# Strassen-form MLP kernel on one core: the last group's last two products made block by block, and three halves of the last norm finished on ScalarE and GpSimd

## The chip, the cores and the metric

The kernel runs on one core of one Trainium2 chip. The metric is the device time of one execution, in microseconds (us). Engines are named as the profile names them: PE is the matrix engine (TensorE) and PEld its weight loads, DVE is VectorE, ACT is ScalarE, POOL is GpSimd, and SP issues the DMA transfers. All times inside an execution are counted from the first instruction of the profiled one.

## What is computed

One layer of a decoder trunk on 512 positions of width 1024, all in float32: three mixers, their gated merge and projection, a first layer norm, then the part that matters here, an MLP with squared ReLU and a second layer norm.

```python
x = _layer_norm(ALPHA * x + mixed, ln1_g, ln1_b)
h = jnp.square(jax.nn.relu(jnp.einsum('bsd,df->bsf', x, w_up)))
x = _layer_norm(ALPHA * x + jnp.einsum('bsf,fd->bsd', h, w_down), ln2_g, ln2_b)

def _layer_norm(x, g, b):
    mu = jnp.mean(x, axis=-1, keepdims=True)
    var = jnp.mean(jnp.square(x - mu), axis=-1, keepdims=True)
    return (x - mu) * lax.rsqrt(var + LN_EPS) * g + b
```

## The kernel before

**Numbers in two parts.** A float32 matmul is made as three matmuls of values split into a high and a low part (`three`, L1246 to L1250). ACT writes the high part of a weight slab, DVE subtracts to get the low part, and PE waits for the low part (`slab`).

**The down product.** The 512 positions are four blocks of 128 (b = 0 to 3), and the 1024 output columns are two halves of 512 (e = 0, 1). Residual and output live in `resid[:, b, half]`. The hidden width of 4096 is worked through in four groups (g = 0 to 3). In each group the down product is a Strassen form with seven products in the order `PRODUCTS`, that is m1, m5, m6, m3, m2, m7, m4. Each product has two row blocks (r = 0, 1), and each row block is one call of `down_part`: four pairs times three matmuls, 12 matmuls of 512 columns. It is written here as "m7,0" for product m7, row block 0.

**Sums in PSUM.** A product that is not in `DOWN_OPENS` goes on adding to the bank that the product before it left: m1, m6, m7 and m4 share bank 4 + r. After each part DVE adds the bank, or subtracts it, into a half of the residual (`down_add`, L1148). So m4,r may not start before DVE has read what m7,r left (`LAST_READ`, `down_ready`: `pe.wait_ge(down_read, made(g, LAST_READ[name], r))`). `made` numbers the parts in the order in which PE makes them, and DVE reads them in that same order. By `down_add`, m3 goes into half 1 of blocks 2 and 3 and m2 into their half 0; m7 goes into half 1 of blocks 0 and 1 and m4 into their half 0.

**The last norm.** In the last group `half_stats` takes the statistics of a half as soon as it is final (L1154). `norm_two(n, b)` then finishes a block: aggregate the statistics (L1157), subtract the mean and multiply with the gain for each half (L1160), take the reciprocal of the standard deviation, of which ACT made the root (L633), then multiply with it and add the bias for each half (L1165). The blocks are finished in the order 2, 3, 0, 1, all on DVE. SP stores each half, 256 KB, in that order (L394).

**Order.** Each engine runs its own instructions strictly in the order in which they are written; there are no priorities. Counting semaphores order the engines among each other.

Of the kernel before, what the change touches and what calls it, by code (L numbers as in the profile page):

```python
# [20 lines left out]
ALU = mybir.AluOpType  # L21
# [8 lines left out]
WID = 512  # L30
# [49 lines left out]

def made(g, name, r):

    return 2 * len(PRODUCTS) * g + 2 * PRODUCTS.index(name) + r + 1


def down_slab(g, name):
# [36 lines left out]
def build(nc, x, mem, lower_bounds, w_in, conv_w, hg_norm_w, w_mem_k, w_mem_v, w_branch, b_gate, w_o,  # L123
          ln1_g, ln1_b, w_up, w_down, ln2_g, ln2_b, out):
    ds = bass.ds
    with ExitStack() as ctx:
# [3 lines left out]
        def sem(name):  # L130
            return ctx.enter_context(nc.semaphore(name))
# [119 lines left out]
        h_squared, form_step, forms_made = sem("h_squared"), sem("form_step"), sem("forms_made")  # L251
        forms_hi, forms_ready = sem("forms_hi"), sem("forms_ready")
        kept_hi, kept_ready = sem("kept_hi"), sem("kept_ready")
        down_done, down_read = sem("down_done"), sem("down_read")

        OPERANDS = 10


        def proj_round(half):
# [53 lines left out]
        def _(sp):  # L313
# [57 lines left out]
            for g in range(G_MLP):  # L371
# [15 lines left out]
                up_load(g, 2)  # L387
                up_load(g, 3)
                direct(g, 4, down_block(g, 2, 1), PAIRS)
            for n, b in enumerate((2, 3, 0, 1)):  # L390
                for e in range(2):
                    part = slice(e * WID, (e + 1) * WID)
                    sp.wait_ge(y_ready, 2 * n + (e + 1))
                    sp.dma_start(out_t[b][:, part], resid[:, b, part]).then_inc(stored, 16)  # L394
            sp.wait_ge(stored, 16 * 2 * TB)


        @block.gpsimd
        def _(pool):
            chain = [0]  # L400

            def after(ins):

                ins.then_inc(pool_chain, 1)
                chain[0] += 1
                pool.wait_ge(pool_chain, chain[0])

            after(pool.memset(ident[:], 0.0))
            pool.affine_select(out=ident[:], in_=ident[:], compare_op=ALU.not_equal, fill=1.0, base=0,
                               pattern=[[-1, P]], channel_multiplier=1).then_inc(ident_ready, 1)  # L410
            after(pool.memset(ones_f, 1.0))
            pool.tensor_copy(ones[:], ones_f)
            pool.memset(scan_keep[:], 1)
            pool.memset(eps[:, 0:1], LN_EPS)
            pool.memset(eps[:, 1:2], RMS_EPS)
            pool.memset(sc_causal, 0.0)
            pool.memset(decays[:, :, 0:1], 1.0)
            after(pool.memset(causal_f, 0.0))

            pool.memset(scan_keep[:].rearrange("p (n c) -> p n c", c=C)[:, :, 0:1], 0)  # L420

            after(pool.affine_select(out=causal_f, in_=causal_f, compare_op=ALU.is_gt, fill=1.0, base=0,
                                     pattern=[[-1, P]], channel_multiplier=1))
            pool.tensor_copy(causal[:], causal_f).then_inc(consts_ready, 1)

            for half in range(2):
                def parts(src, high, low, n, ready):
                    pool.tensor_copy(high, src).then_inc(half_hi, 1)
                    pool.wait_ge(half_hi, n)
                    pool.tensor_tensor(low, src, high.bitcast(F32), ALU.subtract).then_inc(ready, 1)  # L430

                if half == 0:
                    for t in range(4):
                        main_copied(pool, 0, t)
                else:
                    pool.wait_ge(aux_done, HALF.done("as3", half - 1))
                parts(mem_k[:, 2 * half:2 * half + 2, :], mk_hi, mk_lo, 2 * half + 1, khalf_ready)
                if half == 0:  # L440
                    for t in range(4, 8):
                        main_copied(pool, 0, t)
                else:
                    pool.wait_ge(aux_done, HALF.done("pv1", half - 1))
                parts(mem_v[:, :, half * 256:(half + 1) * 256], mv_hi, mv_lo, 2 * half + 2, vhalf_ready)

            pool.wait_ge(branch_split, 8)
            pool.memset(merged, 0.0).then_inc(merge_done, 1)

            for b in range(TB):  # L450
                pool.wait_ge(aux_done, LNT.done("x%d1" % b))
                pool.tensor_scalar(resid[:, b, :], resid[:, b, :], ALPHA, 1.0, ALU.mult, ALU.mult)\
                    .then_inc(resid_ready, 1)


        @block.scalar
        def _(act):
# [249 lines left out]
            def mlp(g):  # L707
                if g == 0:
                    up_hi(0, 2)
                up_hi(g, 3)  # L710
                for j in range(PAIRS):
                    even_tile(g, j)
                    odd_tile(g, j)
                    if j < 3:
                        down_hi(g, PRODUCTS[j])
                    forms_to_hi(g, j)
                down_hi(g, "m3")
                down_hi(g, "m2")
                act.activation(form_hi[:, FORM_OF["m4"], :], h_kept.rearrange("p j t -> p (j t)"), ACT.Copy)\
                    .then_inc(kept_hi, 1)  # L720
                down_hi(g, "m7")
                down_hi(g, "m4")
                if g < G_MLP - 1:
                    for j in range(3):
                        up_hi(g + 1, j)
                else:
                    for n in range(TB):
                        norm(TB + n)

            for g in range(G_MLP):  # L730
                mlp(g)
# [3 lines left out]
        def _(dve):  # L735
# [286 lines left out]
            def half_of(b, e):  # L1022
                return resid[:, b, e * WID:(e + 1) * WID]
# [129 lines left out]
                dve.wait_ge(down_read, made(g, name, r))  # L1153
                ln_link(dve.bn_stats(half_two(b, e), half_of(b, e)))  # L1154

            def norm_two(n, b):
                dve.bn_aggr(mv[:], both_two(b)).then_inc(var_ready, 1)  # L1157
                dve.wait_ge(var_ready, TB + n + 1)
                for e in range(2):
                    dve.scalar_tensor_tensor(half_of(b, e), half_of(b, e), mv[:, 0:1],  # L1160
                                             ln_par[:, 2, e * WID:(e + 1) * WID], ALU.subtract, ALU.mult)
                dve.wait_ge(std_ready, TB + n + 1)
                ln_link(dve.reciprocal(lnw[:, 1:2], lnw[:, 0:1]))
                for e in range(2):
                    dve.scalar_tensor_tensor(half_of(b, e), half_of(b, e), lnw[:, 1:2],  # L1165
                                             ln_par[:, 3, e * WID:(e + 1) * WID], ALU.mult, ALU.add)\
                        .then_inc(y_ready, 1)

            def mlp(g, last):
                if g == 0:  # L1170
# [19 lines left out]
                down_lo(g, "m7")  # L1190
                down_add(g, "m6", 1)
                down_add(g, "m3", 0)
                if last:
                    half_stats(g, "m3", 0)
                down_lo(g, "m4")
                down_add(g, "m3", 1)
                if last:
                    half_stats(g, "m3", 1)
                else:
                    up_lo(g + 1, 0)  # L1200
                down_add(g, "m2", 0)
                if last:
                    half_stats(g, "m2", 0)
                    norm_two(0, 2)
                down_add(g, "m2", 1)
                if last:
                    half_stats(g, "m2", 1)
                else:
                    up_lo(g + 1, 1)
                for r in range(2):  # L1210
                    down_add(g, "m7", r)
                if last:
                    norm_two(1, 3)
                    half_stats(g, "m7", 0)
                    half_stats(g, "m7", 1)
                else:
                    up_lo(g + 1, 2)
                for r in range(2):
                    down_add(g, "m4", r)
                    if last:  # L1220
                        half_stats(g, "m4", r)
                        norm_two(2 + r, r)

            for g in range(G_MLP):
                mlp(g, g == G_MLP - 1)
# [3 lines left out]
        def _(pe):  # L1229
# [350 lines left out]
            def down(g):  # L1580
                for name in ("m1", "m5"):
                    slab(down_slab(g, name))
                    for r in range(2):
                        down_ready(g, name, r)
                        for j in range(PAIRS - 1):
                            pe.wait_ge(forms_ready, PAIRS * g + j + 1)
                            down_part(g, name, r, (j,))
                pe.wait_ge(forms_ready, PAIRS * (g + 1))
                for name in ("m1", "m5"):
                    for r in range(2):  # L1590
                        down_part(g, name, r, (PAIRS - 1,)).then_inc(down_done, 1)
                for name in PRODUCTS[2:]:
                    slab(down_slab(g, name))
                    if name == "m4":
                        pe.wait_ge(kept_ready, g + 1)
                    for r in range(2):
                        down_ready(g, name, r)
                        down_part(g, name, r, range(PAIRS)).then_inc(down_done, 1)

            for g in range(G_MLP):  # L1600
                for u in range(MAIN if g == 0 else 0, 8):
# [25 lines left out]
```

## Time and profile before

| | us |
|---|---|
| time, median of 3 runs | 847.06 (846.89 to 848.33) |
| time of the profiled execution | 847.29 |
| its span, first to last instruction | 845.5 |
| PE busy in the span | 823.7 (97%) |
| DVE busy | 502.7 (59%) |
| ACT busy | 348.0 (41%) |
| POOL busy | 20.3 (2%) |

The span is what the trace can explain. The profiled execution took 1.79 us more than its span, and 0.23 us more than the median of the runs. Shares of busy time are means over the whole kernel; the change touches only the last 30 us, and those are to be read by themselves.

### The profile page before, as it was taken

Reading aid. Unit: us, or ns where it says so; the run is one execution under the profiler, and the core shown is the slowest. Engines: PE = TensorE matmul, PEld = TensorE weight load, DVE = VectorE, ACT = ScalarE, POOL = GpSimd, SP = SyncE. Lnnn points to the kernel's source line nnn. Section 1 sums busy time; section 2 is a strip of 40 time slices with the busy share of each in tenths; the row PEclk is TensorE's granted clock in tenths of the full one; section 3 lists DMA queues with packets and bytes.
Section 4 is the critical chain, followed back from the end, with each engine's and each line's share of the span. In section 5 each row is a group of like instructions: output and inputs, shape, how many; then the busy total and the mean of one; then the engine's idle time right before and its main releaser. Section 6 shows DMA issues by size and latency. Waiting matters only on the chain.

```text
span 845.5 us, 10120 instructions
## 1 busy us (share of the span) xinstructions
PE 823.7 (97%) x4089; PEld 697.2 (82%) x4089; DVE 502.7 (59%) x553; ACT 348.0 (41%) x390; POOL 20.3 (2%) x30
## 2 busy tenths in 40 slices
PE   6999999999999999999999999999999999999994
PEld 6989888889888888888888889878887888788873
DVE  3737635567355514424428685986569566947698
ACT  3739324484236233222225024653544345435430
POOL 1200100000001000000000000000000000000000
PEclk9999999999999999999999999999999999999997
DMA  9541312312033332322732407018102810270002
GB/s 323 178 147 51 100 50 76 118 54 87 12 99 99 101 100 99 99 99 99 292 105 85 164 4 247 0 50 297 52 0 62 291 45 1 95 254 0 1 1 100
DMA packets 67095, 87.52 MB, mean 104 GB/s; under 512 B 1485, under 2 KB 50678, under 8 KB 67062
## 3 DMA queue, kind: packets, MB, share of 16 engines
q1 hardware_dynamic: 67062, 87.06, 30.5%
q8 instruction: 23, 0.38, 0.2%
q14 instruction: 10, 0.08, 0.0%
HBM read 84.96 MB, written 2.10 MB: 103 GB/s over the span
## 4 chain that ended last, share of the span: by engine, by line
PE 96%; DVE 3%; DMA 0%; issue 0%; ACT 0%; DVEq 0%
PE bank L1248 31%; PE bank L1250 30%; PE bank L1249 30%; PE bank L1395 1%; DVE small L1111 1%; DVE two L1148 1%; DVE two L1160 1%; DMA two<-in_mem_dram 0%; PE bank L1440 0%; PE bank L1391 0%; PE bank L1508 0%; PE bank L1361 0%; PE bank L1277 0%; PE bank L1269 0%; DVE smx L1154 0%; PE bank L1443 0%
## 5 line engine op out<-in xcount | busy, mean ns | idle before, releaser
L1248 PE MATMUL bank<-x_hi,w_hi 128*128 128x512 f32 (+1 forms) x704 | 269.7, 383 | 0.0
L1250 PE MATMUL bank<-x_hi,w_lo 128*128 128x512 f32 (+1 forms) x704 | 267.6, 380 | 0.0
L1249 PE MATMUL bank<-x_lo,w_hi 128*128 128x512 f32 (+1 forms) x704 | 267.6, 380 | 0.0
L742 DVE TENSOR_TENSOR w_lo<-raw,w_hi 128x2048 fp32r<-128x2048 f32 x43 | 98.4, 2291 | 115.0 <-ACT w_hi L464 114.7
L1250 PEld LDWEIGHTS bank<-x_hi,w_lo 128*128 128x128 f32 x704 | 132.5, 188 | 25.0
L1249 PEld LDWEIGHTS bank<-x_lo,w_hi 128*128 128x128 f32 x704 | 132.6, 188 | 24.0
L1248 PEld LDWEIGHTS bank<-x_hi,w_hi 128*128 128x128 f32 x704 | 132.6, 188 | 24.0
L1248 PE MATMUL bank<-w_hi,y_hi 128*128 128x512 f32 (+1 forms) x320 | 121.9, 381 | 3.3 <-DVE two L1148 3.3
L1250 PE MATMUL bank<-w_hi,y_lo 128*128 128x512 f32 (+1 forms) x320 | 121.3, 379 | 0.0
L1249 PE MATMUL bank<-w_lo,y_hi 128*128 128x512 f32 (+1 forms) x320 | 121.3, 379 | 0.0
L464 ACT ACTIVATE w_hi<-raw 128x2048 fp32r<-128x2048 f32 x43 | 82.2, 1916 | 52.3 <-PE bank L1250 36.8
L1248 PEld LDWEIGHTS bank<-w_hi,y_hi 128*128 128x128 f32 x320 | 60.2, 188 | 15.8 <-issue 4.9
L1250 PEld LDWEIGHTS bank<-w_hi,y_lo 128*128 128x128 f32 x320 | 60.2, 188 | 11.2
L1249 PEld LDWEIGHTS bank<-w_lo,y_hi 128*128 128x128 f32 x320 | 60.3, 188 | 11.1
L652 ACT ACTIVATE w_hi<-raw 128x2048 fp32r<-128x2048 f32 x18 | 34.5, 1918 | 62.3 <-PE bank L1250 33.6
L747 DVE TENSOR_TENSOR w_lo<-raw,w_hi 128x2048 fp32r<-128x2048 f32 (+1 forms) x20 | 43.7, 2183 | 24.6 <-ACT w_hi L652 24.4
L747 DVE TENSOR_TENSOR w_lo<-small,w_hi 128x2048 fp32r<-128x2048 f32 x24 | 55.0, 2291 | 1.7
L652 ACT ACTIVATE w_hi<-small 128x2048 fp32r<-128x2048 f32 x24 | 45.7, 1904 | 12.9 <-PE bank L1250 12.9
L611 ACT ACTIVATE two<-bank,par 128x512 f32<-128x512 f32 x24 | 16.4, 689 | 81.7 <-PE bank L1250 81.6
L1248 PE MATMUL bank<-y_hi,w_hi 128*128 (+1 forms) x128 | 47.4, 370 | 2.0 <-DVE w_lo L747 2.0
L1249 PE MATMUL bank<-y_lo,w_hi 128*128 (+1 forms) x128 | 47.1, 368 | 0.0
L1250 PE MATMUL bank<-y_hi,w_lo 128*128 (+1 forms) x128 | 47.1, 368 | 0.0
(178 smaller groups left out, 835.3 us busy)
## 6 DMA issues: line engine op xcount, KB each, us to landing
raw<-in_w_in_dram SPq DMA_DIRECT2D x28, 1024.0 KB, 5.0
raw<-in_w_up_dram SPq DMA_DIRECT2D x16, 1024.0 KB, 7.3
small<-in_w_down_dram SPq DMA_DIRECT2D x12, 1024.0 KB, 7.0
raw<-in_w_branch_dram SPq DMA_DIRECT2D x6, 1024.0 KB, 4.9
two<-in_x_dram SPq DMA_DIRECT2D x2, 2048.0 KB, 12.3
raw<-in_w_o_dram SPq DMA_DIRECT2D x4, 1024.0 KB, 5.0
raw<-in_w_down_dram SPq DMA_DIRECT2D x4, 1024.0 KB, 4.6
raw<-in_w_mem_v_dram SPq DMA_DIRECT2D x2, 1024.0 KB, 8.1
```

What stands on the lines that cost most here:

```text
L464: act.activation(w_hi[:, slot, :], raw[:, r, :], ACT.Copy).then_inc(slab_hi, 1)
L611: act.activation(tiles4[:, t, :], main_of(act, rnd, 8 * h + t), ACT.Sigmoid, bias=par[:, ds(i * 8 + (4 * h + t), 1)]).then_inc(main_read[t ...
L652: act.activation(w_hi[:, (s - S_MLP) % 4, :], src, ACT.Copy).then_inc(slab_hi, 1)
L742: dve.tensor_tensor(w_lo[:, slot, :], raw[:, r, :], w_hi[:, slot, :].bitcast(F32), ALU.subtract)\
L747: return dve.tensor_tensor(dst, src, high.bitcast(F32), ALU.subtract)
L1111: dve.tensor_tensor(to, to, other, ALU.add).then_inc(sums_made, 1)
L1148: dve.tensor_tensor(z, z, bank[DOWN_BANK[name] + r], op).then_inc(down_read, 1)
L1160: dve.scalar_tensor_tensor(half_of(b, e), half_of(b, e), mv[:, 0:1], ln_par[:, 2, e * WID:(e + 1) * WID], ALU.subtract, ALU.mult)
L1248: pe.matmul(dst, a[0], b[0], start=first, stop=False, skip_group_check=goes_on)
L1249: pe.matmul(dst, a[0], b[1], start=False, stop=False, skip_group_check=goes_on)
L1250: return pe.matmul(dst, a[1], b[0], start=False, stop=last, skip_group_check=goes_on)
L1395: mm = pe.matmul(t[0:q * C, now], keys, qq[:, h, now], start=True, stop=True)
```

## The change

Three things change in the last group, and nothing before it.

1. PE makes the last two products block by block: m7,0, m4,0, m7,1, m4,1 in place of m7,0, m7,1, m4,0, m4,1. `made` numbers them in the new order.
2. Three halves of the last norm, those in `ON_POOL` (block 2 both halves, block 3 half 0), leave DVE. DVE makes the reciprocal `rstd` and a column `shift`, minus mean times `rstd`; ACT makes z * rstd + shift (Identity with two pointer operands); POOL multiplies with the gain and adds the bias, as two instructions. The statistics' results get a place of their own for each block (`last_of`).
3. DVE's steps are written in a new order (`last_blocks`), and SP stores the three POOL halves first.

```diff
 def made(g, name, r):
+    before = 2 * len(PRODUCTS) * g
+    if g == G_MLP - 1 and name in PRODUCTS[5:]:
+        return before + 10 + 2 * r + PRODUCTS.index(name) - 5 + 1
+    return before + 2 * PRODUCTS.index(name) + r + 1
...
+        LAST = (2, 3, 0, 1)
+        ON_POOL = ((2, 0), (2, 1), (3, 0))
+        def last_of(b):
+            return [decays[:, b, n:n + w] for n, w in ((0, 2), (2, 1), (3, 1), (4, 1))]
...
+            for n, (b, e) in enumerate(ON_POOL):
+                sp.wait_ge(y_pool, n + 1)
+                store(b, e)
+            for n, (b, e) in enumerate(((3, 1), (0, 0), (0, 1), (1, 0), (1, 1))):
+                sp.wait_ge(y_ready, n + 1)
+                store(b, e)
...
+            for n, (b, e) in enumerate(ON_POOL):
+                z = resid[:, b, e * WID:(e + 1) * WID]
+                pool.wait_ge(scaled, n + 1)
+                after(pool.tensor_tensor(z, z, ln_par[:, 2, e * WID:(e + 1) * WID], ALU.mult))
+                pool.tensor_tensor(z, z, ln_par[:, 3, e * WID:(e + 1) * WID], ALU.add).then_inc(y_pool, 1)
...
+            def norm_two(n, b):
+                both_of, std, rstd, shift = last_of(b)
+                act.wait_ge(var_ready, TB + n + 1)
+                act.activation(std, both_of[:, 1:2], ACT.Sqrt, bias=eps[:, 0:1]).then_inc(std_ready, 1)
+                for e in range(2):
+                    if (b, e) in ON_POOL:
+                        z = resid[:, b, e * WID:(e + 1) * WID]
+                        act.wait_ge(scale_ready, n + 1)
+                        act.activation(z, z, ACT.Identity, bias=shift, scale=rstd).then_inc(scaled, 1)
...
+            def aggregate(n, b):
+                dve.bn_aggr(last_of(b)[0], both_two(b)).then_inc(var_ready, 1)
+            def centre(n, b, e):
                 dve.wait_ge(var_ready, TB + n + 1)
+                dve.scalar_tensor_tensor(half_of(b, e), half_of(b, e), last_of(b)[0][:, 0:1],
+                                         ln_par[:, 2, e * WID:(e + 1) * WID], ALU.subtract, ALU.mult)
+            def invert(n, b, shifts):
+                both_of, std, rstd, shift = last_of(b)
                 dve.wait_ge(std_ready, TB + n + 1)
+                ln_link(dve.reciprocal(rstd, std))
+                if shifts:
+                    dve.scalar_tensor_tensor(shift, both_of[:, 0:1], -1.0, rstd, ALU.mult, ALU.mult)\
+                        .then_inc(scale_ready, 1)
+            def finish(b, e):
+                dve.scalar_tensor_tensor(half_of(b, e), half_of(b, e), last_of(b)[2],
+                                         ln_par[:, 3, e * WID:(e + 1) * WID], ALU.mult, ALU.add)\
+                    .then_inc(y_ready, 1)
...
+            def last_blocks(g):
+                for r in range(2):
+                    half_stats(g, "m3", r)
+                down_add(g, "m2", 0)
+                half_stats(g, "m2", 0)
+                aggregate(0, 2)
+                invert(0, 2, True)
+                down_add(g, "m2", 1)
+                half_stats(g, "m2", 1)
+                aggregate(1, 3)
+                centre(1, 3, 1)
+                invert(1, 3, True)
+                down_add(g, "m7", 0)
+                half_stats(g, "m7", 0)
+                finish(3, 1)
+                for n, b in ((2, 0), (3, 1)):
+                    if b:
+                        down_add(g, "m7", b)
+                        half_stats(g, "m7", b)
+                    down_add(g, "m4", b)
+                    half_stats(g, "m4", b)
+                    aggregate(n, b)
+                    for e in range(2):
+                        centre(n, b, e)
+                    invert(n, b, False)
+                    for e in range(2):
+                        finish(b, e)
...
+                for name in PRODUCTS[2:5]:
+                    product(name, range(2))
+                for blocks in ((range(2),) if g < G_MLP - 1 else ((0,), (1,))):
+                    for name in PRODUCTS[5:]:
+                        product(name, blocks)
```

## Rows read from the trace of the kernel before

**Rows 1.** The page's engine line: busy us, share of the span, instructions.

```profile
PE 823.7 (97%) x4089; PEld 697.2 (82%) x4089; DVE 502.7 (59%) x553; ACT 348.0 (41%) x390; POOL 20.3 (2%) x30
```

**Rows 2.** The chain that ended last, 826 to 846 us: start, us, what.

```profile
828.70 0.69 DVE two L1148
...
842.37 0.66 DVEq L126
```

**Rows 3.** DVE in order of time, the end: start, us, engine, line, operation, tiles.

```profile
821.58 0.69 DVE L1154 BATCH_NORM_STATS2 decay<-two 128x6 f32<-128x512 f32 x1
822.31 0.21 DVE L1157 BATCH_NORM_AGGREGATE mv<-decay 128x2 f32<-128x12 f32 x1
822.56 1.41 DVE L1160 SCALAR_TENSOR_TENSOR two<-two,mv,small 128x512 f32<-128x512 f32 x2
823.89 0.15 DVE L1163 RECIPROCAL lnw<-lnw 128x1 f32<-128x1 f32 x1
824.08 1.42 DVE L1165 SCALAR_TENSOR_TENSOR two<-two,lnw,small 128x512 f32<-128x512 f32 x2
825.41 0.68 DVE L1148 TENSOR_TENSOR two<-two,bank 128x512 f32<-128x512 f32 x1
826.12 0.69 DVE L1154 BATCH_NORM_STATS2 decay<-two 128x6 f32<-128x512 f32 x1
...
838.41 0.68 DVE L1148 TENSOR_TENSOR two<-two,bank 128x512 f32<-128x512 f32 x1
```

**Rows 4.** PE in order of time: restart before m6,0, end of m7,1, last matmul.

```profile
806.57 0.47 PE L1248 MATMUL bank<-w_hi,y_hi 128*128 128x512 f32 x1 [0.82 <-DVE two L1148]
806.88 0.40 PE L1249 MATMUL bank<-w_lo,y_hi 128*128 128x512 f32 x1
...
828.22 0.39 PE L1250 MATMUL bank<-w_hi,y_lo 128*128 128x512 f32 x1
...
828.45 0.39 PE L1248 MATMUL bank<-w_hi,y_hi 128*128 128x512 f32 x1
...
833.66 0.39 PE L1250 MATMUL bank<-w_hi,y_lo 128*128 128x512 f32 x1
```

**Rows 5.** POOL in order of time, four of its instructions over 128x512 or more.

```profile
25.75 1.30 POOL L430 TENSOR_TENSOR y_lo<-small,y_hi 128x512 fp32r<-128x512 f32 x1
39.72 1.25 POOL L428 CAST y_hi<-small 128x512 fp32r<-128x512 f32 x1 [12.67 <-ACT small L498]
41.05 1.29 POOL L430 TENSOR_TENSOR y_lo<-small,y_hi 128x512 fp32r<-128x512 f32 x1
...
477.61 1.05 POOL L452 TENSOR_SCALAR two<-two 128x1024 f32<-128x1024 f32 x1 [208.48 <-PE bank L1508]
```

**Rows 6.** DVE in order of time, beside those POOL instructions.

```profile
25.26 2.48 DVE L747 TENSOR_TENSOR x_lo<-bank,x_hi 128x512 fp32r<-128x512 f32 x4
...
38.21 2.29 DVE L742 TENSOR_TENSOR w_lo<-raw,w_hi 128x2048 fp32r<-128x2048 f32 x1 [2.77 <-ACT w_hi L464]
...
41.47 0.90 DVE L784 TENSOR_TENSOR lbw<-lbw 128x4 f32<-128x4 f32 x1
42.40 0.16 DVE L786 TENSOR_TENSOR lbw<-lbw 128x4 f32<-128x4 f32 x1
...
478.37 0.82 DVE L1033 SCALAR_TENSOR_TENSOR two<-two,mv,small 128x512 f32<-128x512 f32 x1
```

**Rows 7.** ACT groups by form: count, then busy us and mean ns.

```profile
L524 ACT ACTIVATE two<-two,lbw 128x512 f32<-128x512 f32 x4 | 3.0, 809 | 0.0
...
L519 ACT ACT_TABLE_LOAD x2 | 2.6, 1283 | 0.0
```

**Rows 8.** ACT in order of time: a root, and the copy behind it.

```profile
478.37 0.29 ACT L633 ACTIVATE lnw<-mv,eps 128x1 f32<-128x1 f32 x1 [7.87 <-DVE mv L1030]
478.57 1.07 ACT L638 ACTIVATE x_hi<-bank 128x512 fp32r<-128x512 f32 x2
```

**Rows 9.** Half-microsecond stretches: PE, PEld, DVE, ACT, POOL busy, granted clock, DMA.

```profile
836.50:837.00 0.50, 0.00 (x0) 0.00 (x0) 0.50 (x2) 0.00 (x0) 0.00 (x0) 1.00 0.00 0
837.00:837.50 0.50, 0.00 (x0) 0.00 (x0) 0.46 (x2) 0.00 (x0) 0.00 (x0) 0.50 0.00 0
```

More of the change, by code:

```diff
@@ L81, in made @@
 def made(g, name, r):
-    return 2 * len(PRODUCTS) * g + 2 * PRODUCTS.index(name) + r + 1
+    before = 2 * len(PRODUCTS) * g
+    if g == G_MLP - 1 and name in PRODUCTS[5:]:
+        return before + 10 + 2 * r + PRODUCTS.index(name) - 5 + 1
+    return before + 2 * PRODUCTS.index(name) + r + 1
 def down_slab(g, name):
@@ L253, in build @@
         kept_hi, kept_ready = sem("kept_hi"), sem("kept_ready")
+        scale_ready, scaled, y_pool = sem("scale_ready"), sem("scaled"), sem("y_pool")
         down_done, down_read = sem("down_done"), sem("down_read")
         OPERANDS = 10
+        LAST = (2, 3, 0, 1)
+        ON_POOL = ((2, 0), (2, 1), (3, 0))
+        def last_of(b):
+            return [decays[:, b, n:n + w] for n, w in ((0, 2), (2, 1), (3, 1), (4, 1))]
         def proj_round(half):
@@ L389, in _, with store @@
                 direct(g, 4, down_block(g, 2, 1), PAIRS)
[L390 to L394, printed above, removed]
+            def store(b, e):
+                part = slice(e * WID, (e + 1) * WID)
+                sp.dma_start(out_t[b][:, part], resid[:, b, part]).then_inc(stored, 16)
+            for n, (b, e) in enumerate(ON_POOL):
[4 more added lines that the diff above has]
+                store(b, e)
             sp.wait_ge(stored, 16 * 2 * TB)
@@ L726, in mlp @@
                 else:
-                    for n in range(TB):
-                        norm(TB + n)
+                    for n, b in enumerate(LAST):
+                        norm_two(n, b)
+            def norm_two(n, b):
[7 more added lines that the diff above has]
+                        act.activation(z, z, ACT.Identity, bias=shift, scale=rstd).then_inc(scaled, 1)
             for g in range(G_MLP):
@@ L1154, in half_stats @@
                 ln_link(dve.bn_stats(half_two(b, e), half_of(b, e)))
-            def norm_two(n, b):
-                dve.bn_aggr(mv[:], both_two(b)).then_inc(var_ready, 1)
+            def aggregate(n, b):
+                dve.bn_aggr(last_of(b)[0], both_two(b)).then_inc(var_ready, 1)
+            def centre(n, b, e):
                 dve.wait_ge(var_ready, TB + n + 1)
-                for e in range(2):
-                    dve.scalar_tensor_tensor(half_of(b, e), half_of(b, e), mv[:, 0:1],
-                                             ln_par[:, 2, e * WID:(e + 1) * WID], ALU.subtract, ALU.mult)
+                dve.scalar_tensor_tensor(half_of(b, e), half_of(b, e), last_of(b)[0][:, 0:1],
+                                         ln_par[:, 2, e * WID:(e + 1) * WID], ALU.subtract, ALU.mult)
+            def invert(n, b, shifts):
+                both_of, std, rstd, shift = last_of(b)
                 dve.wait_ge(std_ready, TB + n + 1)
[L1163 to L1167, printed above, removed]
+                ln_link(dve.reciprocal(rstd, std))
[6 more added lines that the diff above has]
+                    .then_inc(y_ready, 1)
             def mlp(g, last):
@@ L1192, in mlp @@
                 down_add(g, "m3", 0)
-                if last:
-                    half_stats(g, "m3", 0)
                 down_lo(g, "m4")
@@ L1197, in mlp @@
                 if last:
-                    half_stats(g, "m3", 1)
-                else:
-                    up_lo(g + 1, 0)
+                    last_blocks(g)
+                    return
+                up_lo(g + 1, 0)
                 down_add(g, "m2", 0)
-                if last:
-                    half_stats(g, "m2", 0)
-                    norm_two(0, 2)
                 down_add(g, "m2", 1)
[L1206 to L1209, printed above, removed]
+                up_lo(g + 1, 1)
                 for r in range(2):
                     down_add(g, "m7", r)
[L1212 to L1217, printed above, removed]
+                up_lo(g + 1, 2)
                 for r in range(2):
                     down_add(g, "m4", r)
-                    if last:
-                        half_stats(g, "m4", r)
-                        norm_two(2 + r, r)
+            def last_blocks(g):
[25 more added lines that the diff above has]
+                        finish(b, e)
             for g in range(G_MLP):
@@ L1591, in down, with product @@
                         down_part(g, name, r, (PAIRS - 1,)).then_inc(down_done, 1)
-                for name in PRODUCTS[2:]:
+                def product(name, blocks):
                     slab(down_slab(g, name))
@@ L1595, in down @@
                         pe.wait_ge(kept_ready, g + 1)
-                    for r in range(2):
+                    for r in blocks:
                         down_ready(g, name, r)
                         down_part(g, name, r, range(PAIRS)).then_inc(down_done, 1)
+                for name in PRODUCTS[2:5]:
[3 more added lines that the diff above has]
+                        product(name, blocks)
             for g in range(G_MLP):
```

## The prediction

> **What bounds the kernel now.** I read the page's engine line first [rows 1]: PE is busy 97% of the span, so a change in its last 30 us is worth only what it moves at the very end. The chain that ended last says what that is. From 828.70 us on it holds no PE at all, only DVE steps down to the last store's issue, and DVE hands over after 842.37 + 0.66 = 843.03 [rows 2]. PE's last matmul begins at 833.66 and ends at 834.05 [rows 4]. DVE adds that product (m4,1) only at 838.41 [rows 3], 4.3 us late, because it is still finishing blocks 3 and 0. So the end is set by DVE's queue. The last store then takes 845.5 - 843.03 = 2.5 us, before and after.
>
> **Prices on DVE.** All from start to start in [rows 3]: an add or a statistics step 0.71 to 0.73, aggregate 0.25, two passes over a half each 1.33 (so one is 0.665), reciprocal 0.19. Add, statistics and a whole norm are 0.71 + 0.73 + 0.25 + 1.33 + 0.19 + 1.33 = 4.54; from the last add to the hand-over the trace has 843.03 - 838.41 = 4.62.
>
> **What DVE saves.** Three halves lose both passes: 6 x 0.665 = 4.0 us. Two `shift` steps come in, one column each, 0.2 apiece if nothing holds them. Net some 3.6 us of DVE work, nearly the 4.3 us by which the last add is late. If DVE's load were all that counted, the end would now hang on PE.
>
> **What the new order on PE costs.** Before, m7,1 runs between m7,0 and m4,0, so DVE can read bank 4 meanwhile; m4,0 follows m7,1 without a gap, 828.22 to 828.45 [rows 4]. Now m4,0 stands right behind m7,0 in the same bank and needs DVE's read of it, and m4,1 needs that of m7,1. One such wait: matmul 0.39, hand-over to DVE 0.09 (828.61 to 828.70), add 0.69, back to PE about 0.14, less the 0.23 that the next matmul would have waited anyway: 1.1 us. The restart shows a first step of 0.31 in place of 0.23 [rows 4]. A part of 12 matmuls is 12 x 0.227 = 2.72 us; from its first matmul after a gap to DVE's add it is 0.31 + 10 x 0.227 + 0.39 + 0.09 = 3.05 us.
>
> **Where DVE's order puts the second wait.** This decides the sum. In `last_blocks` the add of m7,1 stands behind everything of block 0, its two `finish` passes too. DVE runs in order, so PE holds m4,1 until block 0's norm is over, though m7,1 has long been made. The end of the kernel is now one serial chain: add m7,0, part m4,0, add and norm of block 0, add m7,1, part m4,1, add and norm of block 1.
>
> Its shortest form: m7,0 ends 2.72 before m7,1's 828.61, at 825.89, and its add begins at 825.98. PE restarts 0.69 + 0.14 later, at 826.81. DVE adds m4,0 at 829.86, and block 0 is done 4.54 later, at 834.40. The add of m7,1 lets PE go at 835.23; the last add is at 838.28, against 838.41 now. The 4 us of freed DVE time come back as waits, and 0.1 us is left. This is the bound from below.
>
> **What POOL adds.** POOL now runs six tensor_tensor over 128x512, and the trace has that instruction at 1.29 to 1.30 [rows 5]. Beside POOL some DVE instructions stand still. A 128x4 tensor_tensor on DVE takes 0.16 by itself, but 0.90 when it starts at 41.47: it ends at 42.37, just behind POOL's at 42.34 [rows 5, 6]. DVE's pass at 478.37 took 0.82 and ended at 479.19, 0.53 behind POOL's 478.66, as if its 0.665 step, less a lead of 0.13, had begun only when POOL was through. The other way round, POOL's cast at 39.72 took 1.25 and ended 0.47 behind DVE's subtraction of two SBUF tensors (40.50). Four DVE subtractions with one operand in PSUM ran at 0.62 each across POOL's work at 25.75. So a `centre`, `finish` or `shift`, with two SBUF operands, takes turns with POOL's instruction; adds and statistics do not. The Trainium skill says as much (GPSIMD Engine Reference, Key points: contention comes "with DVE instructions in a 2-port perf mode or with two SBUF inputs"), and gives no price. By it alone the sum would stay between the bound above and the one below, which is made from the rows.
>
> Walked through (estimates):
> - `rstd` and `shift` of block 2 are made at 822.7 to 823.05, ahead of any POOL work. ACT's pass with two pointer operands is 0.81 [rows 7]: scaled halves at 823.9 and 824.6.
> - POOL's multiply 1 runs 823.95 to 825.25. DVE's `centre` of block 3 begins 824.95, streams from 825.25, ends 825.8. POOL's second instruction waits for it and holds until about 826.95.
> - DVE's `shift` of block 3, a single column, comes up at 825.9 and stands until 826.97. Behind it in DVE's queue is the add of m7,0, for which PE waits. It starts at 827.0, not at 825.98: **1.0 us late on the chain**.
> - POOL's next two run to 829.7. `finish(3,1)`, up at 828.45, ends at 830.2, before m4,0 is ready for its add at 830.9. Hidden, with 0.7 to spare.
> - POOL's sixth ends at about 832.8; block 0's `centre` comes up at 832.5 and loses 0.1.
> - The other passes run beside an idle POOL. The first stores are far from the end.
>
> The sum: -0.13 (bound) + 1.0 (`shift`) + 0.1 (`centre`) = about +0.9 us, last add at 839.3. In the profile's own terms 847.29 + 0.9 = 848.2; against the median, 847.06 + 0.9 = 847.95. The bounds of the POOL term: 0 if `shift` slips in between two POOL instructions; 1.1 for `shift` and up to 1.1 more for `centre`, if POOL's sixth is later than I put it. That makes -0.1 to +2.1, 846.9 to 849.2. I take 1.0 since every POOL instruction is followed at once by another there.
>
> **Costed at nothing.** ACT's three passes lie beside DVE's statistics; ACT is otherwise idle there. If they were 0.5 us longer, the root for block 3 would be late and `invert` with it. The low part of m4's slab moves forward by one statistics step, and PE needs it only at 826. Identity stands in no row. A Copy follows a root at once, 478.37 to 478.57 [rows 8], while a table load is 1.28 [rows 7]. The Trainium skill (ScalarE: Activation LUTs, Table sets: the hidden batching unit) says that the cheap functions are in every set, which would make it 0 for Identity too.
>
> **Rivals.**
> 1. *The granted clock falls in PE's new gap.* PE ends m7,1 at 833.6 and starts m4,1 at about 836.3, idle for 2.7 us, after an earlier gap of 1.9. Before, the clock fell from 1.00 to 0.50 (2.4 to 1.2 GHz) at 837.0 [rows 9], 2.95 us after the last matmul ended. At 1.2 GHz 512 columns take 0.427 in place of 0.227: 12 x 0.2 = +2.4 us on the chain, if all of m4,1 is slow. Then 850.3, and from a half-slow m4,1 upwards (+1.2, 849.2) it is slower than 0.2%. For it: 2.7 is close to 2.95. Against it: it is below it, and after the gap of 0.82 at 806.57 the matmuls ran at 0.40 as elsewhere [rows 4]. 20%.
> 2. *POOL costs nothing*: -0.1, 846.9. For it: it needs only a lucky slot for a 0.2 us instruction. Against it: POOL's instructions follow each other within 0.1. 20%.
> 3. *POOL costs more*, the 1.1 of `centre` on top, or Identity needs a table load each way (1.28 before the passes and again before the root of block 3, some 1.3 us more on `invert`): 849.0 to 849.4, slower. 10%.
> 4. *The change does what its parts would do alone*: DVE is free when each product ends and PE's two gaps of 1.1 are all. Last add 834.14 + 2.2 = 836.3, that is -2.1, 844.95, faster. It needs the add of m7,1 ahead of block 0's passes, and the code has it behind. 3%.
>
> My forecast, +0.9, has the remaining 47%.
>
> **The numbers.** 847.9 us. The 8 in 10 range takes in the rival without POOL's cost and most of the clock's: 846.7 to 850.2. The likeliest case's own is 847.2 to 848.8. A measurement here can't tell 0.2%, 1.7 us, from no change. Within it lie the forecast, rival 2 and part of rivals 1 and 3: 0.70. Slower by more: most of rivals 1 and 3 and the edge of the forecast: 0.26. Faster by more: rival 4 and a little for what I overlooked: 0.04.
>
> **What would show it.** In the profile after: two PE idles before L1248 matmuls released by DVE L1148's line, near 1.9 and 2.7 us; the second part of bank 5 begun only after the passes of block 0; one-column DVE steps of which that of block 3 takes about 1 us, and no other; the clock at 1.00 until after the last matmul; DVE's last add at 839.3; no table load in the last 25 us. If `shift` is short, the forecast is 1.0 too high. If PE's second gap is 1 us, I misread the order. If the matmuls of m4,1 step at 0.43, rival 1 holds.

## The result, and the profile after

The changed kernel takes 849.48 us (median of 11 runs, 847.92 to 849.83) against 847.06 for the kernel before (11 runs, 846.75 to 848.33). The ratio is 1.0023, with a 95% interval of 1.0015 to 1.0032: it is slower. The profiled execution took 849.70 with a span of 847.9, and both stand 2.4 us above the kernel before (847.29 and 845.5).

In short, and shown by the runs below: the saved DVE work is there, the new order of the products gives it back, and the granted clock of PE takes more on top. DVE's timeline of the changed kernel, columns as in [rows 3]:

```profile
824.86 0.85 DVE L1195 SCALAR_TENSOR_TENSOR two<-two,decays,small 128x512 f32<-128x512 f32 x1
...
825.82 1.03 DVE L1203 SCALAR_TENSOR_TENSOR decays<-decays 128x1 f32<-128x1 f32 x1
826.77 0.67 DVE L1182 TENSOR_TENSOR two<-two,bank 128x512 f32<-128x512 f32 x1
827.48 0.69 DVE L1188 BATCH_NORM_STATS2 smx<-two 128x6 f32<-128x512 f32 x1
828.21 1.78 DVE L1207 SCALAR_TENSOR_TENSOR two<-two,decays,small 128x512 f32<-128x512 f32 x1
830.65 0.69 DVE L1182 TENSOR_TENSOR two<-two,bank 128x512 f32<-128x512 f32 x1 [0.66 <-PE bank L1305]
...
832.35 1.42 DVE L1195 SCALAR_TENSOR_TENSOR two<-two,decays,small 128x512 f32<-128x512 f32 x2
833.68 0.16 DVE L1201 RECIPROCAL decays<-decays 128x1 f32<-128x1 f32 x1
833.87 1.41 DVE L1207 SCALAR_TENSOR_TENSOR two<-two,decays,small 128x512 f32<-128x512 f32 x2
835.20 0.68 DVE L1182 TENSOR_TENSOR two<-two,bank 128x512 f32<-128x512 f32 x1
...
840.82 0.69 DVE L1182 TENSOR_TENSOR two<-two,bank 128x512 f32<-128x512 f32 x1 [4.20 <-PE bank L1305]
```

Read it from the bottom. The last add (m4,1) comes at 840.82 after DVE has stood idle for 4.20 us, waiting for PE. In [rows 3] that add came at 838.41 and DVE never waited for it. PE in turn waited for the add at 835.20, that of m7,1, which stands behind the two passes at 833.87. And the one-column `shift` at 825.82 takes 1.03 us. The reason is in POOL's timeline: its second instruction was held up itself, by DVE's pass over block 3 (`centre`, at 824.86), and runs until 826.83.

```profile
823.87 1.30 POOL L476 TENSOR_TENSOR two<-two,small 128x512 f32<-128x512 f32 x1 [312.21 <-ACT two L762]
825.24 1.59 POOL L477 TENSOR_TENSOR two<-two,small 128x512 f32<-128x512 f32 x1
```

PE's timeline shows both gaps, and what came after the second (compare the one restart in [rows 4]):

```profile
825.40 0.39 PE L1305 MATMUL bank<-w_hi,y_lo 128*128 128x512 f32 x1
827.59 0.47 PE L1303 MATMUL bank<-w_hi,y_hi 128*128 128x512 f32 x1 [1.80 <-DVE two L1182]
...
832.88 0.39 PE L1305 MATMUL bank<-w_hi,y_lo 128*128 128x512 f32 x1
836.03 0.47 PE L1303 MATMUL bank<-w_hi,y_hi 128*128 128x512 f32 x1 [2.76 <-DVE two L1182]
836.34 0.40 PE L1304 MATMUL bank<-w_lo,y_hi 128*128 128x512 f32 x1
836.57 0.39 PE L1305 MATMUL bank<-w_hi,y_lo 128*128 128x512 f32 x1
836.80 0.48 PE L1303 MATMUL bank<-w_hi,y_hi 128*128 128x512 f32 x1
837.08 0.63 PE L1304 MATMUL bank<-w_lo,y_hi 128*128 128x512 f32 x1
837.50 0.63 PE L1305 MATMUL bank<-w_hi,y_lo 128*128 128x512 f32 x1
```

m4,1 starts at steps of 0.23. From 837.08 on a matmul takes 0.63 and the next follows 0.42 later. The windows view has the granted clock at 1.00 and then 0.50, that is 2.4 and then 1.2 GHz:

```profile
836.50:836.95 0.45, 0.45 (x3) 0.36 (x3) 0.11 (x1) 0.00 (x0) 0.00 (x0) 1.00 0.85 319
837.00:837.50 0.50, 0.50 (x2) 0.33 (x1) 0.00 (x0) 0.00 (x0) 0.00 (x0) 0.50 0.00 0
```

The gap was 2.76 us long, and the clock fell at 837.0, 0.9 us after PE had started again; in [rows 9] it fell after PE had ended for good.

### The profile page after: what moved, and what is told of

Same layout as the page of the kernel before. It is cut to its first block, busy times and chain, and to the rows that moved or that the text cites. A ratio compares the mean times of both kernels' runs of the same rounds, so it can differ in the third digit from the quotient of the medians.

```text
span 847.9 us, 10125 instructions
## 1 busy us (share of the span) xinstructions
PE 825.8 (97%) x4089; PEld 697.6 (82%) x4089; DVE 500.8 (59%) x549; ACT 350.4 (41%) x393; POOL 28.7 (3%) x36
## 4 chain that ended last, share of the span: by engine, by line
PE 96%; DVE 3%; DMA 0%; issue 0%; ACT 0%; DVEq 0%
PE bank L1303 31%; PE bank L1304 30%; PE bank L1305 30%; PE bank L1450 1%; DVE small L1145 1%; DVE two L1182 1%; DMA two<-in_mem_dram 0%; DVE two L1195 0%; PE bank L1495 0%; PE bank L1446 0%; PE bank L1563 0%; PE bank L1416 0%; PE bank L1332 0%; PE bank L1324 0%; PE bank L1498 0%
```

## How the runs are compared

Executions differ before the changed part begins: m5 ends up to 1.7 us earlier or later (804.85 to 806.51 in the table). So each profile is read against its own last matmul of m5, the point just before [rows 4] begins (805.36 in the kernel before). The **tail** is the time from there to the start of DVE's last add. From that add to the end all these kernels do the same, but for `old_order_wide`. "Falls" says that the granted clock went to 0.50 (1.2 GHz) during m4,1. The last column has the median time, and in brackets that of the kernel before, measured beside it.

| kernel | last matmul of m5 | last add | tail | second PE gap | clock in m4,1 | median (before, same chip) |
|---|---|---|---|---|---|---|
| before | 805.36 | 838.41 | 33.05 | none | 1.00 | |
| changed | 805.26 | 840.82 | 35.56 | 2.76 | falls | 849.48 (847.06) |
| same_again_1 | 805.39 | 839.33 | 33.94 | 2.75 | 1.00 | one run, 848.20 |
| same_again_2 | 805.29 | 840.86 | 35.57 | 2.75 | falls | one run, 849.72 |
| fill_gap | 804.85 | 838.81 | 33.96 | filled | 1.00 | 848.73 (847.38) |
| add_early | 805.62 | 837.93 | 32.31 | 1.22 | 1.00 | 846.70 (847.38) |
| pool_one_column | 805.24 | 839.94 | 34.70 | 2.75 | falls | 848.97 (847.38) |
| pe_order_alone | 805.52 | 841.58 | 36.06 | 3.25 | falls | 850.21 (847.16) |
| both_repairs | 806.51 | 840.29 | 33.78 | 1.92 | falls | 847.86 (847.16) |
| both_repairs_filled | 805.33 | 837.48 | 32.15 | 0.34 left | 1.00 | 846.39 (847.35) |
| old_product_order | 805.08 | 835.80 | 30.72 | none | 1.00 | 844.93 (847.38) |
| old_order_wide | 806.17 | 836.75 | 30.58 | none | 1.00 | 844.87 (847.35) |

## The experiments

**fill_gap.** In the changed kernel PE gets twelve matmuls that nobody reads, in place of the second wait.

```diff
+                        if g == G_MLP - 1 and name == "m4" and 1 in blocks:
+                            pe.wait_ge(up_read, 8 * G_MLP)
+                            for n in range(12):
+                                pe.matmul(bank[2], form_hi[:, FORM_OF["m7"], 0:P],
+                                          w_hi[:, (down_slab(g, "m7") - S_MLP) % 4, 0:WID], start=True, stop=True)
                         product(name, blocks)
```

> Twelve matmuls that nobody reads fill PE's wait between m7,1 and m4,1 in the changed kernel; they write a bank that is free by then. Theory (the granted clock falls because PE stands still there, and that is the larger part of the loss): clock 1.00 up to the last matmul, the matmuls of m4,1 step at 0.227 throughout, DVE's last add at 839.1 in place of 840.8, median 1.5 to 2.0 us below the changed kernel, near 847.8. Rival (the clock falls for another reason, or the loss lies in waits): it falls all the same, median near 849.5. If the filler ends late it delays m4,1 by at most 0.3 us.

PE's timeline, the filler and the start of m4,1:

```profile
832.68 2.88 PE L1662 MATMUL bank<-w_hi,y_hi 128*128 128x512 f32 x12
835.59 0.47 PE L1303 MATMUL bank<-w_hi,y_hi 128*128 128x512 f32 x1
835.90 0.40 PE L1304 MATMUL bank<-w_lo,y_hi 128*128 128x512 f32 x1
836.13 0.40 PE L1305 MATMUL bank<-w_hi,y_lo 128*128 128x512 f32 x1
```

The steps stay at 0.23 and the tail is 33.96, 1.6 less than in the changed kernel's profile, though PE does more. The median fell by only 0.75, half of the least that was expected (against the kernel before, from 2.42 above to 1.35 above); its ratio to before is 1.0012 (1.0003 to 1.0022). The profiled execution, at 847.70, was the fastest of eleven, and the slowest took 849.63. So the clock costs less on average than in that one profile, or it does not fall in every execution. The next two runs test that. Another reading stays untested: the filler leaves the first gap, of 1.80 us, and the clock may fall there in some executions; none of the slower ones was profiled.

**same_again_1 and same_again_2.** The changed kernel, unedited.

> The changed kernel once more, nothing edited: one more profiled execution. Theory (the fall of the clock in PE's 2.76 us gap is a matter of the single execution, and so the median is less than the profile's 1.7 us above full clock): PE's steps and gaps as before, and in some executions m4,1 steps at 0.227 throughout (last add 33.8 us behind the last matmul of m5), in others at 0.43 for up to eight matmuls (35.6 us behind). Rival: it falls in each, always 35.6 us.

> As the run before it: a third profiled execution of the changed kernel. Theory: the last add lies between 33.8 and 35.6 us behind the last matmul of m5, not the same in each. Rival: 35.6 again.

Both outcomes occurred, with PE gaps equal to 0.01 us. In same_again_1 the matmuls of m4,1 stayed at full rate and the tail is 33.94; in same_again_2 they slowed and it is 35.57. PE's timeline in the first of the two:

```profile
836.16 0.47 PE L1303 MATMUL bank<-w_hi,y_hi 128*128 128x512 f32 x1 [2.75 <-DVE two L1182]
836.46 0.40 PE L1304 MATMUL bank<-w_lo,y_hi 128*128 128x512 f32 x1
...
838.51 0.39 PE L1304 MATMUL bank<-w_lo,y_hi 128*128 128x512 f32 x1
```

and in the second:

```profile
836.08 0.47 PE L1303 MATMUL bank<-w_hi,y_hi 128*128 128x512 f32 x1 [2.75 <-DVE two L1182]
...
837.01 0.63 PE L1303 MATMUL bank<-w_hi,y_hi 128*128 128x512 f32 x1
```

The same program with the same gap loses 1.6 us or nothing, from one execution to the next. Without the fall the change costs 33.94 - 33.05 = 0.89 us.

**add_early.** One edit in DVE's order.

```diff
                     for e in range(2):
                         centre(n, b, e)
+                    if b == 0:
+                        down_add(g, "m7", 1)
+                        half_stats(g, "m7", 1)
                     invert(n, b, False)
```

(The two calls ahead of the add of m4,1 are gone.)

> The changed kernel with one edit: DVE adds m7,1 before block 0's reciprocal and last two passes, not behind them. Theory (the second wait of PE comes from DVE's order): PE's second gap shrinks from 2.8 to about 1.4 us, the clock stays at 1.00, last add near 837.6, median near 846.3, which is 0.1% below the kernel before. Rival (the gap is the price of two products in one bank, whatever DVE's order): the gap stays near 2.8 and the time near 849.5.

PE's second restart in its timeline:

```profile
834.86 0.47 PE L1303 MATMUL bank<-w_hi,y_hi 128*128 128x512 f32 x1 [1.22 <-DVE two L1182]
835.16 0.40 PE L1304 MATMUL bank<-w_lo,y_hi 128*128 128x512 f32 x1
```

The gap went from 2.76 to 1.22 (1.4 expected), the clock stayed, and the tail is 32.31, 1.63 below the changed kernel's at full clock, 33.94 (1.5 expected). The ratio to before is 0.9988 (0.9979 to 0.9997): with this one move the slower kernel is a slightly faster one.

**pool_one_column.** POOL's six instructions work on one column each.

```diff
-                z = resid[:, b, e * WID:(e + 1) * WID]
+                z = resid[:, b, e * WID:e * WID + 1]
```

(The slices of `ln_par` are cut in the same way.)

> The changed kernel with POOL's six instructions cut to one column each, so gain and bias are left out in the rest of three halves. Theory (a DVE step with two SBUF operands takes turns with POOL's): shift of block 3 takes 0.16 in place of 1.03, the add of m7,0 starts at 826.0 in place of 826.8, the chain behind it is 0.8 to 0.9 us earlier; PE's second gap keeps its 2.8 us, so the clock may fall as before, and the median is near 848.6. Rival (the step is long by itself or waits for something else): it stays at 1.0 and the median near 849.5.

DVE's timeline:

```profile
825.70 0.16 DVE L1203 SCALAR_TENSOR_TENSOR decays<-decays 128x1 f32<-128x1 f32 x1
825.86 0.69 DVE L1182 TENSOR_TENSOR two<-two,bank 128x512 f32<-128x512 f32 x1
826.58 0.69 DVE L1188 BATCH_NORM_STATS2 smx<-two 128x6 f32<-128x512 f32 x1
827.31 0.75 DVE L1207 SCALAR_TENSOR_TENSOR two<-two,decays,small 128x512 f32<-128x512 f32 x1
```

`shift` takes 0.16 in place of 1.03 and the pass behind it 0.75 in place of 1.78. The add of m7,0 comes at 825.86, 0.91 earlier, and the tail is 0.86 below the changed kernel's with a fallen clock, 34.70 against 35.56. The median, 848.97, is 1.59 above the kernel before in place of 2.42. The clock fell here too, from the second matmul of m4,1 on, and was back before the part had ended. PE's timeline:

```profile
835.15 0.50 PE L1303 MATMUL bank<-w_hi,y_hi 128*128 128x512 f32 x1 [2.75 <-DVE two L1182]
...
835.87 0.63 PE L1305 MATMUL bank<-w_hi,y_lo 128*128 128x512 f32 x1
...
838.86 0.41 PE L1303 MATMUL bank<-w_hi,y_hi 128*128 128x512 f32 x1
```

**pe_order_alone.** The kernel before with PE's new order; DVE does the whole norm, and adds m7,1 behind block 0's norm as in the changed kernel.

```diff
+                if last:
+                    down_add(g, "m7", 0)
+                    norm_two(1, 3)
+                    half_stats(g, "m7", 0)
+                    for r in range(2):
+                        if r:
+                            down_add(g, "m7", 1)
+                            half_stats(g, "m7", 1)
+                        down_add(g, "m4", r)
+                        half_stats(g, "m4", r)
+                        norm_two(2 + r, r)
+                    return
```

(`made` and PE's loop are those of the changed kernel.)

> The kernel before with PE's new product order alone, every half of the norm on DVE as before. Theory (the order costs by itself, since DVE adds m7,1 only behind block 0's norm): add m7,0 at 826.9, block 0 done at 835.9, PE's second gap 3.4 us, last add at 839.8 with the clock at 1.00 and up to 2.4 later if it falls; median 1.4 to 3.5 us above the kernel before. Rival (with all work on DVE the order doesn't matter, since DVE is the bound anyway): last add at 838.4, median unchanged.

PE's second restart in its timeline:

```profile
836.79 0.73 PE L1255 MATMUL bank<-w_hi,y_hi 128*128 128x512 f32 x1 [3.25 <-DVE two L1151]
```

The ratio is 1.0032 (1.0020 to 1.0043), the slowest of all: tail 36.06, gap 3.25, clock fallen. PE restarted at 836.79, and 3.05 from there, the prediction's price at full clock, would give 839.84 (839.8 expected) and a tail of 34.3, so the order costs about 1.3 before the clock's part. The order alone makes the loss; the new division of the norm wins some of it back.

**both_repairs.** add_early, and the add of m7,0 ahead of block 3's reciprocal.

```diff
-                invert(1, 3, True)
                 down_add(g, "m7", 0)
+                invert(1, 3, True)
                 half_stats(g, "m7", 0)
```

> The changed kernel with two moves in DVE's order: the add of m7,0 ahead of block 3's reciprocal and shift, and the add of m7,1 ahead of block 0's reciprocal. Theory: the 0.8 us of the first and the 1.5 us of the second add up; last add 31.5 us behind the last matmul of m5 where the kernel before has 33.05, both PE gaps under 1.4 us, clock at 1.00, median near 846.0, still 1 us above the version with the old product order. Rival (the moved reciprocal makes the finish of block 3 late, and block 0 with it): no more than add_early gave, near 846.7.

This missed. The ratio is 1.0007 (0.9997 to 1.0016) and the runs spread from 845.91 to 849.32. Counted from the last matmul of m5, the add of m7,0 came 0.9 us earlier (20.62 against 21.51) and block 0's `centre` 0.8 earlier (26.25 against 27.09), but POOL's last instruction only 0.1 (25.86 against 25.96). So DVE's passes now ran into it. POOL's timeline, and DVE's:

```profile
832.37 1.29 POOL L477 TENSOR_TENSOR two<-two,small 128x512 f32<-128x512 f32 x1
```

```profile
832.76 2.11 DVE L1195 SCALAR_TENSOR_TENSOR two<-two,decays,small 128x512 f32<-128x512 f32 x2
834.79 0.67 DVE L1182 TENSOR_TENSOR two<-two,bank 128x512 f32<-128x512 f32 x1
```

The two passes took 2.11 in place of 1.42, so the second gap became 1.92 where add_early had 1.22, and the clock fell 0.5 us after PE had started again. PE's timeline:

```profile
835.61 0.47 PE L1303 MATMUL bank<-w_hi,y_hi 128*128 128x512 f32 x1 [1.92 <-DVE two L1182]
...
836.56 0.63 PE L1303 MATMUL bank<-w_hi,y_hi 128*128 128x512 f32 x1
```

With 3.05 from 835.61 the last add would be at 838.66, an estimated tail of 32.15 at full clock.

**both_repairs_filled.** The same with seven filler matmuls before m4,1, as in fill_gap.

> Both moves in DVE's order, and seven matmuls that nobody reads between m7,1 and m4,1 on PE. Theory (both_repairs lost its gain to the clock, which fell in a gap of 1.9 us, and to block 0's passes that now wait 0.7 for POOL): clock at 1.00 in the profile, last add 32.2 us behind the last matmul of m5, median 1 to 1.5 us below both_repairs, near 846.6. Rival (the moves themselves cost, whatever the clock): last add 33 us behind or more, median near 847.9.

Tail 32.15, clock 1.00, median 846.39, all 11 runs within 845.97 to 847.24. So the moves were worth only 0.16 more than add_early (32.31), and it was the clock that took both_repairs' gain, where 5 of 12 runs had taken 849.17 or more. Seven matmuls that nobody reads make that kernel 1.5 us faster by its medians, 847.86 and 846.39, and 1.7 us if each is counted from the kernel before it (0.70 above, 0.96 below).

**old_product_order.** The new division of the norm with the old order on PE.

```diff
-                for blocks in ((range(2),) if g < G_MLP - 1 else ((0,), (1,))):
-                    for name in PRODUCTS[5:]:
-                        product(name, blocks)
+                for name in PRODUCTS[5:]:
+                    product(name, range(2))
...
                 finish(3, 1)
+                down_add(g, "m7", 1)
+                half_stats(g, "m7", 1)
```

(`made` is the old one, and the two calls are gone from the loop.)

> The norm's new division of work kept, PE's new order undone (m7,0, m7,1, m4,0, m4,1 as before); DVE adds m7,1 behind the first half that it finishes. Theory (DVE's saved work is real and the block by block order throws it away): no PE gap after m7,0, last add near 836.0 in place of 838.4, median 2.4 us below the kernel before, near 844.7. Rival (the new division itself saves nothing, because DVE stands still beside POOL): last add at 838 or later, median 847 or more.

Tail 30.72, 2.33 below before (2.4 expected); median 844.93, ratio 0.9968 (0.9956 to 0.9980). With the new division of the norm, then, PE's new order costs 1.6 even with the add of m7,1 early (add_early, 32.31) and 3.2 with it late (33.94). DVE's timeline has no pause from the add of m4,0 on, while POOL costs it the same as in the changed kernel:

```profile
825.64 1.06 DVE L1201 SCALAR_TENSOR_TENSOR decays<-decays 128x1 f32<-128x1 f32 x1
...
831.25 0.69 DVE L1180 TENSOR_TENSOR two<-two,bank 128x512 f32<-128x512 f32 x1
...
835.80 0.68 DVE L1180 TENSOR_TENSOR two<-two,bank 128x512 f32<-128x512 f32 x1
```

**old_order_wide.** On top of it, `centre` of blocks 0 and 1 as one instruction over 1024 columns.

```diff
-                    for e in range(2):
-                        centre(n, b, e)
+                    dve.wait_ge(var_ready, TB + n + 1)
+                    dve.scalar_tensor_tensor(resid[:, b, :], resid[:, b, :], last_of(b)[0][:, 0:1],
+                                             ln_par[:, 2, :], ALU.subtract, ALU.mult)
```

> The version with the old product order, and the first pass of blocks 0 and 1 made as one instruction over 1024 columns in place of two over 512. DVE is the bound there from the add of m4,0 on without a pause, so each saved step counts in full: two passes over 512 take 1.33, one over 1024 about 1.2, twice. Theory: last add and end 0.1 and 0.25 us earlier, median near 844.7 against 844.9. Rival (a pass over 1024 is no cheaper, or the root for the reciprocal comes too late): no change.

In the profile the expected 0.25 is there: the 1024-column pass and its step take 1.21 (834.02 to 835.23) where the two took 1.33, so the tail is 0.14 shorter and the stretch behind the last add 0.13. The medians, 844.87 and 844.93, can't tell 0.25 us from nothing; for the time it stays open.

## Why the prediction came out as it did

The forecast of +0.9 us was right in its steps and wrong in what the clock would do; the measured +2.4 is rival 1. The range up to 850.2 holds the 849.48 only because it took in most of that rival, and the outcome given 70%, no more than 1.7 us from the kernel before, did not come; "slower by more", given 26%, did.

- *The shape of the chain.* Right: both PE gaps, at the places named, for the reasons named. The gaps were 1.80 and 2.76 where 1.9 and 2.7 were expected. add_early shows that DVE's order made most of the second gap, and old_product_order that PE's order made the need for either.
- *The bound of -0.1.* Right within 0.1, by an estimate. In pool_one_column the add of m7,1 came at 834.33; with 0.83 to PE's restart and 3.05 for the part, the last add at full clock would be at 838.21, a tail of 32.97 against 33.05. The 3.05 was a little low: in same_again_1 the add came 3.17 after the restart (836.16 to 839.33), since the last matmul ended 0.20 before it and not 0.09.
- *POOL's price, 1.0 on `shift` and 0.1 on `centre`.* Mis-sized by little: `shift` lost 0.87 and with the late pass before it 0.91; `centre` of block 0 lost nothing (1.42). The sum at full clock was +0.89 in same_again_1 and +0.91 in fill_gap, against +0.9. That it fits so well is in part luck: POOL's part came out 0.2 too high and the last part's length 0.1 too low.
- *The clock.* This is the step that failed. Rival 1 had 20%, because 2.7 us of idle time is less than the 2.95 after which the clock had fallen in [rows 9]. The clock fell in two of three profiled executions of the changed kernel, and in both_repairs after a gap of 1.92. One row of one execution told after which idle time the clock had fallen once, not how short a gap is safe. The gap of 0.82 in [rows 4] was no evidence for gaps three times as long. The price per slow matmul, 0.2, held: the difference to a full clock was 1.62 to 1.63 for eight slow matmuls in the changed kernel, from the fifth on. The 2.4 for a wholly slow m4,1 came in no profile, not even in pe_order_alone, where the clock fell with its first matmul: it was back at 1.00 after eight, and the tail stood 1.7 above its estimate at full clock.
- *Identity and the tables.* No table load showed in the last 25 us; ACT's first two passes came 0.72 apart. The term of 0 held.

What stays open: in how many executions the clock falls. Three profiles and eleven times are too few for a share, since executions also differ before the changed part. Open too is why fill_gap's median stands 1.35 above the kernel before, where its profile's tail stands 0.91 above.

## What to carry to other kernels

When an order makes an engine wait for a bank that another engine must read first, ask what stands ahead of that read in the reader's queue: here the product order turned 3.2 us to waits at full clock (a tail of 33.94 against 30.72), 1.6 of them because one add stood behind a norm. Give each PE wait near the end a second price, that of the clock, before calling it hidden, and don't take a gap for safe because it is shorter than the idle time of the one fall on record: that was 2.95 us here, and a gap of 1.92 was followed by a fall too. Work moved to POOL is not free for DVE: count which of DVE's steps have two SBUF operands (here `centre`, `shift` and `finish` were held up beside POOL's instructions, adds of a bank and statistics were not), and which of them stand in front of something that PE waits for.

## What the hardware showed beside that

- A fall of the clock depends on the execution: a gap of 2.75 us was followed by a fall in same_again_2 and not in same_again_1, one of 1.92 was (both_repairs), and one of 1.80 (in fill_gap, ahead of m4,0) was not. Each fall in m4,1 came after PE had started again: at once in pe_order_alone (836.8), 0.3 us later in pool_one_column (835.5), 0.9 in the changed kernel (837.0).
- The start of an execution differs as well. In both_repairs the early 256-column matmuls step at 0.21 until 16.8 us, in fill_gap at 0.12 from 11.3 on, as if the clock rose that much earlier; the granted clock reads 1.00 in both there, so this is argued from the steps alone. m5's last matmul begins at 806.51 and 804.85. Those 1.7 us are most of the 2.1 by which the runs of the kernel before spread (846.61 to 848.69); that the first makes the second is likely and not shown. PE's timeline in both_repairs, and in fill_gap:

```profile
16.56 0.41 PE L1305 MATMUL bank<-y_hi,w_lo 128*128 128x256 f32 x1
16.78 0.37 PE L1303 MATMUL bank<-y_hi,w_hi 128*128 128x256 f32 x1
16.98 0.28 PE L1304 MATMUL bank<-y_lo,w_hi 128*128 128x256 f32 x1
```

```profile
11.28 0.28 PE L1304 MATMUL bank<-y_lo,w_hi 128*128 128x256 f32 x1
11.40 0.28 PE L1305 MATMUL bank<-y_hi,w_lo 128*128 128x256 f32 x1
```

- Taking turns between DVE and POOL goes by instruction, not by element: a step of one column took 0.87 us longer (1.03 against 0.16) and ended at 826.85, when POOL's 512 columns had ended at 826.83. It goes both ways: POOL's own instruction behind `centre` took 1.59 in place of 1.30.
